# Three groups of SBUF buffers moved to start addresses 0, 128 and 256 bytes past a multiple of 512

## What is computed

```python
h = rmsnorm(x, g_mix_pre);  z = h @ w_in            # q, k, v, u, qx, gates
y_attn = sliding_window_attention(rope(q), rope(k), v, sinks)
y_ssm  = s5_branch(u, ...)                          # GELU, then GLU with w_glu
y_mem  = memory_cross_attention(qx, km, vm)         # km, vm = rmsnorm(mem) @ w_mem_kv
merged = sig(g0)*(y_attn @ w_branch_attn) + sig(g1)*(y_ssm @ w_branch_ssm) + sig(g2)*(y_mem @ w_branch_mem)
x = x + rmsnorm(merged @ w_out, g_mix_post)
h = rmsnorm(x, g_mlp_pre)
x = x + rmsnorm(square(relu(h @ w_up)) @ w_down, g_mlp_post)
```

## The kernel before

| buffers | start address | modulo 512 |
|---|---|---|
| raw, whi, wlo | 18720, 35104, 51488 | 288 |
| hThi, hTlo, tok | 67872, 100640, 133408 | 288 |
| rho | 149792 | 288 |
| yst, scr | 149856, 158048 | 352 |
| mThi, mTlo | 178528, 186720 | 352 |
| yhi, ylo, acc | 162144, 178528, 194912 | 352 |

## Time and profile before

### The profile page before, as it was taken

One profiled execution on the slowest core, in us unless ns is written; L12 is line 12 of the kernel. 1 busy time (PEld: TensorE's weight loads), 2 busy tenths in 40 slices (PEclk: granted clock), 3 DMA queues, 4 the chain that ended last, 5 costly groups with the idle time before them and its releaser, 6 DMA issues.

```text
span 1640.7 us, 18345 instructions
## 1 busy us (share of the span) xinstructions
PE 1580.5 (96%) x7423; PEld 1311.9 (80%) x7423; DVE 834.7 (51%) x1590; ACT 431.3 (26%) x588; POOL 120.0 (7%) x193
## 2 busy tenths in 40 slices
PE   4899999999999999999999899999999999999997
PEld 4788768978888888888898788888888888888885
DVE  5839567628458435446766633333333333323348
ACT  5433223232222126221234321212021212111121
POOL 2000000032202212100000200000000000000000
PEclk8899998999999999999999999999999999999998
DMA  7401111242121145414433311110111111111104
GB/s 264 108 26 52 39 63 41 70 110 90 57 91 59 65 116 195 165 47 149 139 118 102 141 52 52 52 51 26 51 51 51 51 51 37 42 49 51 52 1 166
DMA packets 82063, 130.93 MB, mean 80 GB/s; under 512 B 13104, under 2 KB 55120, under 8 KB 82000
## 3 DMA queue, kind: packets, MB, share of 16 engines
q1 hardware_dynamic: 66256, 76.03, 14.3%
q0 software_dynamic: 15744, 54.03, 9.7%
HBM read 104.88 MB, written 25.17 MB: 79 GB/s over the span
## 4 chain that ended last, share of the span: by engine, by line
PE 90%; DVE 6%; DMA 2%; ACT 1%; issue 1%; SPq 0%; DVEq 0%; ACTq 0%
PE bank L1349 83%; DMA raw<-in_w_mem_kv_dram 2%; PE bank L1362 2%; PE bank L1566 1%; PE bank L1454 1%; PE bank L1580 1%; DVE tok L1319 1%; DVE wlo L285 1%; DVE yst L1311 1%; PE bank L1522 0%; DVE acc L1326 0%; PE bank L1549 0%; PE bank L1584 0%; PE bank L1481 0%; DVE prob L944 0%
## 5 line engine op out<-in xcount | busy, mean ns | idle before, releaser
L1349 PE MATMUL bank<-hThi,whi 128*128 128x512 f32 x1184 | 464.7, 393 | 4.4 <-DVE hTlo L1261 1.8
L1349 PE MATMUL bank<-hTlo,whi 128*128 128x512 f32 x1184 | 463.1, 391 | 0.0
L1349 PE MATMUL bank<-hThi,wlo 128*128 128x512 f32 x1184 | 463.1, 391 | 0.0
L1349 PEld LDWEIGHTS bank<-hThi,whi 128*128 128x128 f32 x1184 | 224.0, 189 | 52.5 <-issue 4.3
L1349 PEld LDWEIGHTS bank<-hThi,wlo 128*128 128x128 f32 x1184 | 223.7, 189 | 47.1
L1349 PEld LDWEIGHTS bank<-hTlo,whi 128*128 128x128 f32 x1184 | 223.8, 189 | 46.3
L279 ACT ACTIVATE whi<-raw 128x2048 fp32r<-128x2048 f32 x65 | 124.2, 1911 | 375.0 <-PE bank L1349 343.9
L1349 PE MATMUL bank<-whi,yhi 128*128 128x512 f32 x512 | 202.6, 396 | 0.6 <-DVE wlo L285 0.6
L1349 PE MATMUL bank<-wlo,yhi 128*128 128x512 f32 x512 | 202.5, 395 | 0.0
L1349 PE MATMUL bank<-whi,ylo 128*128 128x512 f32 x512 | 202.5, 395 | 0.0
L285 DVE TENSOR_TENSOR wlo<-raw,whi 128x2048 fp32r<-128x2048 f32 x65 | 148.9, 2291 | 94.9 <-ACT whi L279 94.8
(11 more groups left out here) (306 smaller groups left out, 1841.8 us busy)
## 6 DMA issues: line engine op xcount, KB each, us to landing
raw<-in_w_in_dram SPq DMA_DIRECT2D x34, 512.0 KB, 4.6
raw<-in_w_up_dram SPq DMA_DIRECT2D x32, 512.0 KB, 4.5
raw<-in_w_down_dram SPq DMA_DIRECT2D x32, 512.0 KB, 4.4
gate_scratch<-scr POOLq DMA_DIRECT2D x48, 256.0 KB, 2.3
tok<-gate_scratch POOLq DMA_DIRECT2D x24, 512.0 KB, 3.7
raw<-in_w_mem_kv_dram SPq DMA_DIRECT2D x8, 512.0 KB, 11.9
y_scratch<-yst POOLq DMA_DIRECT2D x16, 256.0 KB, 2.7
yst<-y_scratch POOLq DMA_DIRECT2D x16, 256.0 KB, 4.2
```

The lines of the kernel that those rows point to most:

```text
L1349: ins = T.matmul(dst, lhs(k)[p], rhs(k)[q], start=start and k == 0 and i == 0, stop=stop and k == kt - 1 and i == 2)
```

## The change

The 16 constants of rho are taken before raw instead of after tok, and 160 bytes of pad follow them. Two more pads of 128 bytes are taken, one before hThi and one after scr. No instruction changes; only addresses do.

```diff
--- before.py
+++ after.py
@@ -125,14 +125,16 @@
         smalli = sb("smalli", [P, NPAIR], i32)
         sinkx = sb("sinkx", [P, 16, 4])
         ldt = sb("ldt", [NPAIR, 2])
+        rho = sb("rho", [P, NPAIR])
+        sb("pad", [P, 40])
         raw = sb("raw", [P, 2, UNIT])
         whi = sb("whi", [P, 2, UNIT], f32r)
         wlo = sb("wlo", [P, 2, UNIT], f32r)
 
+        sb("pad1", [P, 32])
         hThi = sb("hThi", [P, KT, L], f32r)
         hTlo = sb("hTlo", [P, KT, L], f32r)
         tok = sb("tok", [P, 4096])
-        rho = sb("rho", [P, NPAIR])
         yst = sb("yst", [P, 4, 512])
 
         yst2 = yst[:, 0:2, :]
@@ -144,6 +146,7 @@
         rotF = cut(592, 224).rearrange("p (a b k) -> p a b k", a=2, b=7)
         small = cut(816, 192).rearrange("p (a k) -> p a k", a=12)
         scr = sb("scr", [P, 2, 512])
+        sb("pad2", [P, 32])
 
         with ExitStack() as att:
             kmT = sb("kmT", [P, XH, MEM], f32, att)
```

## The result

The changed kernel takes 1651.4 us (median of four runs, 1649.9 to 1652.7) where the kernel before takes 1642.1. The ratio is 1.0065, with a 95% interval of 1.0053 to 1.0077: slower by 0.65%, where 1603 had been forecast. The span of its profiled execution is 1647.7 us against 1640.7.

A forecast was written before the change was run, and what follows sets the result against it. PE was taken as the bound, through the distance between its matmuls; 1642.88 us less 39.3 (5890 matmuls at 6.67 ns) gave 1603.6, or 1603.0 as median, other engines costed at nothing; range 1566 to 1658 us.

The forecast's parts named there:

- What bounds the kernel, and how to read it: Whole kernel: PE, busy 1580.5 of 1640.7 us, bounds it through the distance between matmul start times, not mean latency.
- about 60: Matmuls running at half clock, left out of the gain because the surcharge there is nil; their distance should stay 426 ns.
- DVE and the transfers cost nothing: Other engines: DVE costed at nothing, under 1 us if moved 1%; weight DMAs, landing in 4.5 us, cover enough.
- I take one step off every matmul: Matmuls with both operands contiguous: 64-byte alignment saves 6.67 ns on each of 5890, 39.3 us; chance 0.33.
- 33 pieces instead of 32: Operand fetch: starts 32 past a multiple of 64 make 2048 bytes touch an extra 64-byte piece, costing 16 ticks, 6.67 ns.
- The 39.3 us of forecast gain: Up-like, down, merges and output projection: 5890 matmuls times 6.67 ns saved, taking 1642.88 us to 1603.6.
- No effect: Whole kernel: the surcharge belongs to roles and loop shapes, not addresses; time stays at 1642 us; chance 0.17.
- Slower: difference 0 was the best relation: MLP up half and projections: up-like matmuls rise to 233.5 ns, down at 256 stays; 1667.6 us; chance 0.23.
- Only the difference counts, repeating every 256 bytes: Down and merges come to 226.7 ns, up stays; 10.7 us less, 1631.7 us; chance 0.15.
- The floor of 216 ns: Lowest 512-column matmul distance, from the float32 pass's roughly 3 ns of fixed cost over the bare columns.
- all collisions vanish: All matmuls reach the floor of 216 ns, 73.5 us less, 1569 us; chance 0.12.

The follow-up runs named there:

- All at 0: Against the changed kernel, only the first pad kept, so every buffer from raw on begins at 0 modulo 512: 1629.24 us, 0.9925 of the kernel before.
- all at 352: Against the changed kernel, rho ahead of raw and no pads, so every buffer from raw on begins at 352 modulo 512: 1630.49 us.
- at 256: Against the changed kernel, pads changed: raw, whi, wlo at 352, hThi, hTlo, yhi, ylo at 96; up +256, down -256: 1633.5 us.
- both at 224: Against the changed kernel, pads changed: raw, whi, wlo at 0, hThi, hTlo, yhi, ylo at 224 modulo 512: 1669.1 us in one run.
- the kernel with +16 and +48: Against the changed kernel, hThi/hTlo and yhi/ylo made halves of shared buffers, difference +16 in up, +48 in down: 1657.1 us in one run.
- the kernel with +8: Against the changed kernel, hThi/hTlo and yhi/ylo as halves of shared buffers, difference +8 in up, -16 in down: 1663.0 us in one run.

## Why the prediction was wrong

**What bounds the kernel, and how to read it: right.** The distances of start times account for the result. 2016 matmuls of the up kind outside the MLP at 6.0 ns more are 12.1 us; inside, +6.5 and -6.6 ns on 1536 each nearly cancel; the merges give back 384 x 2.2 = 0.8; the output projection adds 288 x 3.5 = 1.0. Together 12.2 us, against 9.3 between the medians and 7.0 between the spans. The 5.2 us missing in the spans can be found, to a few tenths. The first projection starts at 66.59 us before and at 64.08 after, 2.5 us earlier; the granted clock of the first 65 us was 0.87 before and 0.99 after. Later, 34 of the 512-column matmuls of `product` ran at the half clock before (the prediction had put about 60) and 26 after, at about 0.2 us each 1.6 us; their distance stayed at 426 ns. And the 1.4 us in which PE stood idle ahead of merge A did not come again. Nothing ties these three to the places: the mean granted clock, 0.984 before and 0.991 after, went from 0.983 to 0.990 between runs of the kernel before. DVE and the transfers cost nothing, as said.

**The step that failed** is "I take one step off every matmul ... because the 64-byte alignment is the one thing that changes for all of them in the same direction". The size of a step was right, the reason for it was not. The arithmetic (512 + 32, 512 + 48, 256 + 16 ticks) fitted 33 pieces instead of 32, but in the kernel before every start was 32 past a multiple of 64, so no row could tell an alignment cost from any other constant. All at 0 against all at 352 shows that cost to be zero: 226.7 ns in both. The 39.3 us of forecast gain were this term and nothing else. In its place the difference decides: 2016 matmuls outside the MLP went from 226.7 to between 232.4 and 233.3 ns, about 12 us more. That 1651 lies within the range of 1566 to 1658 is luck: the range was wide enough to hold no effect and part of the slower case, while 1603 and a chance of 0.60 for faster were wrong.

**The rivals.** Two of them were each half right, and I had priced them as if they excluded each other. "Slower: difference 0 was the best relation" had the up kind at 233.5 (measured 233.3 in the MLP, 232.4 to 233.3 before it), but left the down half dear. "Only the difference counts, repeating every 256 bytes" had down at 226.7 (measured 226.7), but left up unchanged. Taken together, with the prices that stood in the text: 23.3 + 1.9 - 10.7 = 14.5 us, 1657, slower. The rows gave the half of it: 0 was the cheapest row of 512 columns. That 256 is worth the same and 128 costs a full step stood in no row, but both were already among the rivals. What I lacked was the question which counts the two effects have against each other: 3552 matmuls leave the cheap relation and 1920 (down and merges A and S) enter it. With 0 the cheapest and 256 equal to it, that count alone gives the sign.

"No effect" is excluded by the exchange of the two halves. The Trainium skill ("SBUF — State Buffer", section "Who interferes with whom") calls the two read ports of PE independent. The traces do not agree, as far as time goes: the distance of matmuls moved by up to 6.8 ns in the MLP with nothing changed but the places of the two operands to each other. That PE never waits on another engine, the other half of that rule, is not touched by these runs. The floor of 216 ns, which I had worked out for the case that all collisions vanish, was not seen at any of the differences tried, nor with half a weight load.

**What the prediction named as its test** was fair: "I am wrong if up and down move in opposite directions: then the difference decides and not the alignment." They did.

**What stays open.** Why coincidence is cheap at 512 columns and dear at 256 columns, what the surcharge of 13.4 ns that it leaves is made of, and what picks one of several rhythms. The runs show the rule for the difference and the rhythm, not the mechanism: that the two operands' reads get into each other's way is a guess that fits the dependence on their difference, and no run tests it by itself.

## What to carry to other kernels

Where float32r matmuls of 512 columns follow each other without gaps, give the moving and the stationary operand start addresses that are equal modulo 256 bytes; a small buffer allocated between two large ones can break this, and here 64 bytes of rho cost 11 us of 1642. At 256 columns do not: there nothing tried was dearer than equal addresses. Weigh such a change by how many matmuls of each pairing it moves, all pairings of a buffer counted, since moving one buffer changes every product it takes part in. And a constant that all rows share (here the 32 bytes past 64) is no evidence for its own cost: it takes a run with and without it.

## What the runs showed of the hardware

Mean distance of matmuls of 128 x 128 float32r with 512 columns at a granted clock of 1.00, in settled runs, by moving minus stationary start address modulo 256 (up and down are the halves of the MLP):

| difference | ns | seen in |
|---|---|---|
| 0 | 226.7 | up and down of all at 0, all at 352, and at 256; down after the change; values against activations with both at 224 |
| 8 | 233.4 to 233.5 | up |
| 16 | 231.7 to 231.8 | up; merges |
| 32 | 233.3 | up of one kernel, down of another |
| 48 | 231.9 | down |
| 64 | 228.9 to 229.0 | up and down; merges before |
| 96 | 233.3 | down |
| 128 | 232.4 to 233.3 | up and projections, two kernels |
| 160 | 234.3 | merges |
| 192 | 233.3; 228.9 | down before, merges; the output projection of the kernel with +16 and +48 |
| 208 | 230.0; 234.7 | merge A and merge S of one kernel (+16 and +48) |
| 224 | 233.3 | up |
| 240 | 233.3; 226.7 | down and two groups of the output projection; four groups of it |
| 248 | 230.8 | the output projection of the kernel with +8 |

At 0 the difference fixes the distance. At the others it fixes less: 192, 208 and 240 have two distances several ns apart. At 256 columns the order is another: 120.0 ns at 0, 118.6 at 128, 117.8 at 64, 113.3 at 192.

Multiples of 512 bytes inside the buffers, and the 8 KB between the ring's two slots, left no mark. Some of these distances are a whole number of steps of 6.67 ns (16 ticks of 2.4 GHz) for each group of three matmuls: 680, 687, 693 and 700 ns for 226.7, 228.9, 231.1 and 233.3; others, such as 232.4 and 230.0, are not. I had not expected that the same matmuls at the same places can keep different distances for a whole stage (231.1 and 233.3 ns in two groups of gates of one kernel), nor that halving the weight load would lengthen the distance, from 226.7 to 230.0 ns.
